# Two blocks of a float32 transformer on one core: first units by halves, a low part in two operations, and one load on another queue

## The reference

```python
def first_block(x, ...):                      # two layers
    x = x + 0.5 * swiglu_ffn(rmsnorm(x), ffn1_wi, ffn1_wo)
    z = rmsnorm(x) @ w_in                     # q, k, v, gates, two output gates ga and gb
    yA = (sigmoid(mo) * rmsnorm(mlstm_chunkwise(...))) @ w_a
    yB = swa_sink_attention(...) @ w_b
    mixed = sigmoid(ga) * yA + sigmoid(gb) * yB
    x = x + mixed @ w_out
    x = x + 0.5 * swiglu_ffn(rmsnorm(x), ffn2_wi, ffn2_wo)
    x = x + sigmoid(rmsnorm(x) @ w_ple_gate) * (p @ w_ple)

def second_block(x, ...):                     # two layers
    uv, z, xbc, dt, c_q, c_kv, k_rope = split(rmsnorm_2(x) @ w_in_2)
    y = [gmlp_mixer(uv), ssd_mixer(z, xbc, dt), mla_mixer(c_q, c_kv, k_rope, cos, sin)]
    x = x + concatenate(y) @ w_out_2
    x = x + square(relu(rmsnorm_2(x) @ mlp_w1)) @ mlp_w2
```

## Time and profile before

| | us |
|---|---|
| median of three executions | 3557.78 |
| profiled execution | 3561.82 |
| its span in the trace | 3560.0 |
| TensorE matmuls busy | 3481.5 |
| TensorE weight loads busy | 2786.3 |
| DVE busy | 1766.3 |
| GpSimd busy | 1402.4 |
| ScalarE busy | 1004.3 |

### The profile page before, as it was taken

The page is one execution under the profiler, slowest core; times in us unless marked ns, Lnnn a source line. Parts: engine busy times, 40 slices in busy tenths (PEclk is TensorE's granted clock), DMA queues, the critical chain, the costliest instruction groups (busy, mean ns, idle before and its releaser), DMA issues.

```text
span 3560.0 us, 42975 instructions
## 1 busy us (share of the span) xinstructions
PE 3481.5 (98%) x15538; PEld 2786.3 (78%) x15538; DVE 1766.3 (50%) x2059; ACT 1004.3 (28%) x1290; POOL 1402.4 (39%) x583
## 2 busy tenths in 40 slices
PE   8999999999999999999999999999999999999998
PEld 7888876788888788887678888776788887578887
DVE  5442246654424643133765442568481826848171
ACT  3222233222222322223422222333321123342112
POOL 3444432344443444433234444331244443134442
PEclk9999999999999999999999999999999999999999
DMA  4333322233332333332123333321233323123332
GB/s 143 95 94 101 107 73 58 71 89 100 99 102 84 100 100 95 107 88 77 55 77 95 99 95 103 93 69 34 66 92 97 94 92 85 30 66 101 95 100 78
DMA packets 496142, 311.26 MB, mean 87 GB/s; under 512 B 41784, under 2 KB 454811, under 8 KB 496027
## 3 DMA queue, kind: packets, MB, share of 16 engines
q1 hardware_dynamic: 494460, 307.47, 29.4%
q10 hardware_dynamic: 1567, 2.18, 0.2%
HBM read 305.94 MB, written 3.67 MB: 87 GB/s over the span
## 4 chain that ended last, share of the span: by engine, by line
issue 45%; PE 31%; POOL 20%; DVE 3%; DVEq 1%; POOLq 1%; ACT 0%; DMA 0%; ACTq 0%
POOL wl L480 20%; PE bank L517 5%; PE bank L521 4%; PE bank L498 4%; PE bank L503 4%; PE bank L502 4%; PE bank L523 4%; PE bank L1104 1%; PE mb L1131 1%; PE bank L524 1%; PE mb L568 1%; PE mb L1047 1%; DVE sd_p L2124 0%; POOLq L479 0%; DVE xl L1644 0%
## 5 line engine op out<-in xcount | busy, mean ns | idle before, releaser
L480 POOL TENSOR_TENSOR wl<-raw,wh 128x1024 fp32r<-128x1024 f32 x576 | 1401.6, 2435 | 2119.6 <-ACT wh L1258 2119.5
L1258 ACT ACTIVATE wh<-raw 128x1024 fp32r<-128x1024 f32 x576 | 608.0, 1057 | 1616.0 <-PE bank L498 723.7
L517 PE MATMUL bank<-xh,wh 128*128 128x512 f32 x2400 | 940.9, 392 | 0.0
L521 PE MATMUL bank<-xl,wh 128*128 128x512 f32 x2400 | 936.1, 390 | 0.0
L523 PE MATMUL bank<-xh,wl 128*128 128x512 f32 x2100 | 819.4, 390 | 0.0
L517 PEld LDWEIGHTS bank<-xh,wh 128*128 128x128 f32 x2400 | 451.8, 188 | 102.7 <-issue 9.0
L521 PEld LDWEIGHTS bank<-xl,wh 128*128 128x128 f32 x2400 | 452.0, 188 | 92.8
L498 PE MATMUL bank<-hh,wh 128*128 128x512 f32 (+1 forms) x1216 | 473.2, 389 | 0.0
L503 PE MATMUL bank<-hh,wl 128*128 128x512 f32 (+1 forms) x1216 | 473.0, 389 | 0.0
L502 PE MATMUL bank<-hl,wh 128*128 128x512 f32 (+1 forms) x1216 | 473.0, 389 | 0.0
L523 PEld LDWEIGHTS bank<-xh,wl 128*128 128x128 f32 x2100 | 395.5, 188 | 83.0
(11 more groups left out here) (383 smaller groups left out, 3292.4 us busy)
## 6 DMA issues: line engine op xcount, KB each, us to landing
raw<-in_ffn_wi_dram SPq DMA_DIRECT2D x176, 512.0 KB, 3.7
raw<-in_mlp_w_dram SPq DMA_DIRECT2D x128, 512.0 KB, 3.7
raw<-in_w_in_dram SPq DMA_DIRECT2D x102, 512.0 KB, 3.6
raw<-in_ffn_wo_dram SPq DMA_DIRECT2D x88, 512.0 KB, 3.6
raw<-in_w_out_dram SPq DMA_DIRECT2D x32, 512.0 KB, 3.8
raw<-in_w_ple_gate_dram SPq DMA_DIRECT2D x16, 512.0 KB, 3.7
raw<-in_w_a_dram SPq DMA_DIRECT2D x8, 512.0 KB, 3.3
raw<-in_w_b_dram SPq DMA_DIRECT2D x8, 512.0 KB, 3.3
```

Of the source, the lines that this page charges most:

```text
L480: gp.tensor_tensor(wl[j][:], raw[j % RAW_SLOTS][:], wh[j][:].bitcast(F32), ALU.subtract)\
L517: first = pe.matmul(out[0:width, :], h[:, c:c + width], rh[:, k, :], start=k == 0, stop=False)
L521: pe.matmul(out[0:width, :], h[:, c:c + width], rl[:, k, :], start=False, stop=False)
L1258: act.activation(wh[n % SPLIT_SLOTS][:], raw[n % RAW_SLOTS][:], ACT.Copy).then_inc(s.hi_ready, 1)
```

## The change

Three edits. First, the output projection's units 0 to 3 are written out by halves, in the manner of `first_units` without the sum of squares; each of the eight waits for `mixed_ready` stands in unit 0 of its half. Units 4 to 7 stay plain, and without a wait. Second, GpSimd's subtraction of a slab is two operations of 128x512 with one increment behind the second. Third, the wait on line 385 is gone, and the table's load stands on ScalarE's queue in block 2's first layer, behind the four gelus of `gmlp`.

```diff
@@ sync @@
-            sp.wait_ge(s.tile_evacuated, tiles_out(Block1, 1, T_PLE + 5))
-            sp.dma_start(rope[:], a["rope_pack"]).then_inc(s.rope_landed, 16)
@@ gpsimd @@
                     gp.wait_ge(s.hi_ready, n * SPLIT_SLOTS + j + 1)
-                    gp.tensor_tensor(wl[j][:], raw[j % RAW_SLOTS][:], wh[j][:].bitcast(F32), ALU.subtract)\
-                      .then_inc(s.split_done, 1)
+                    for half in range(2):
+                        part = slice(half * (SLAB // 2), (half + 1) * (SLAB // 2))
+                        last = gp.tensor_tensor(wl[j][:, part], raw[j % RAW_SLOTS][:, part], wh[j][:, part].bitcast(F32),
+                                                ALU.subtract)
+                    last.then_inc(s.split_done, 1)
@@ tensor, gated @@
-                for j in range(KT):
-                    unit(Block1, L, S_OUT + j, T_OUT + j, mh, ml, part_ready=s.mixed_ready,
-                         wait_k=(lambda k: at(L, KT, k + 1)) if j == 0 else None)
+                for half in range(2):
+                    for u in range(4):
+                        n = S_OUT + u
+                        if not half:
+                            take_slab(Block1, L, n)
+                            open_tile(Block1, L, T_OUT + u)
+                        out = bank[(Block1.base_tile + T_OUT + u) % TILE_BANKS][:]
+                        h, l = wh[n % SPLIT_SLOTS], wl[n % SPLIT_SLOTS]
+                        for kt in range(4 * half, 4 * half + 4):
+                            if u == 0:
+                                pe.wait_ge(s.mixed_ready, at(L, KT, kt + 1))
+                            c = kt * P
+                            last = three(out, h[:, c:c + P], l[:, c:c + P], mh[:, kt, :], ml[:, kt, :], kt == 0,
+                                         kt == KT - 1, new=kt == 4 * half and (u > 0) == (half > 0))
+                        if half:
+                            last.then_inc(s.tile_ready, 1)
+                for j in range(4, KT):
+                    unit(Block1, L, S_OUT + j, T_OUT + j, mh, ml)
@@ scalar, gmlp of block 2 @@
                     act.activation(proj2[:, u, :], proj2[:, u, :], ACT.Gelu_apprx_tanh)
+                if L == 0:
+                    act.dma_start(rope[:], a["rope_pack"]).then_inc(s.rope_landed, 16)
                 act.drain()
```

## The result

The changed kernel takes 3528.83 us (median of 6 runs, 3519.3 to 3533.68) where the kernel before took 3556.24 (6 runs, 3553.79 to 3559.77): a ratio of 0.992, 95% interval 0.991 to 0.9929, or about 28 us less. The forecast was 3537, 8 us above it; the measured time lies 0.8 us inside the lower end of the forecast's range of 3528 to 3549. The run profiled took 3528.16 us, its span is 3526.4.

The account below looks back on a forecast made before the run. TensorE, busy 98% of the span, bounds the kernel by its work plus waits. Terms -13.8 - 6.8 + 0 = -20.6 us give 3541.2 from the profiled execution, 3537 by the median; range 3528 to 3549.

Parts of the forecast that it names:

- The projection by halves: Block 1's output projection, both layers: waits for the mixed tiles' low part and half-clock time go, -13.8 us.
- The bank's wait: Output projection, unit 2: opening its bank waits for DVE's read of tile 6; 1.15 us a layer, between 0.8 and 2.
- The first rival: Output projection: openings of units 1 to 3 wait longer and the clock falls; 3543 us, chance 0.13.
- The table's move: Seam between blocks 1 and 2: slab loads no longer queue behind the table's wait on SP; -6.8 us.
- The third rival: Second seam: moving the table's load does nothing, as slab rounding or another load holds it; 3544 us, chance 0.08.
- The split: GpSimd's low parts in two operations: gains and costs where TensorE waits for DVE cancel; 0 us, between -8 and +10.
- The seams: `xl` before the sum of squares, both seams: one waiting operation ends sooner with halved low parts, -0.9 us x 2.
- The chains: Successive waiting DVE operations let GpSimd in once more: logits' scalings +0.3 us at four waits, scan heads' products and query +0.3 x 2.
- The scan: Block 2's first layer: a single DVE operation waiting for GpSimd ends sooner with halved low parts, -1.15 us.
- The added operation: GpSimd's second operation per slab: 0.1 us more a slab at some ten places where TensorE waits on DVE.
- The slower rival: Attention and scan stages: splitting low parts lengthens TensorE's path by 0.45 us at about 80 slabs; 3573 us, chance 0.08.
- the second, 3527: Rival that splitting low parts gains at every place, DVE never meeting the second half; 3527 us, chance 0.10.

Follow-up runs that it names:

- e3: Only the rotary table's load moved to ScalarE's queue, against the kernel before: 3545.18 us, ratio 0.9976.
- e8: All three edits, but the table loaded on SP's queue behind block 2's first four slabs and the gMLP parameters, against the kernel before: 3529.84 us, ratio 0.9923.
- e4: Projection by halves and table's load moved, low parts left whole, against the kernel before: 3537.94 us, ratio 0.9948.
- e10: The changed kernel, all three edits, run again against the kernel before: 3526.57 us, ratio 0.9918.
- e1: Only the output projection's first four units by halves, against the kernel before: 3544.58 us, ratio 0.9966.
- e11: All three edits, but low parts in four uneven operations of 512, 480, 16 and 16 columns, against the kernel before: 3527.38 us, ratio 0.9916.
- e12: All three edits, but low parts in eight operations of 128x128, against the kernel before: 3518.97 us, ratio 0.9897.
- e9: All three edits, but low parts in four operations of 128x256, second run of that kernel, against the kernel before: 3519.57 us, ratio 0.9894.
- e7: All three edits, but low parts in four operations of 128x256, first run of that kernel, against the kernel before: 3521.27 us, ratio 0.9899.

## Why the prediction was off, step by step

**The projection by halves: right, to its size.** -13.8 was forecast, 12 measured alone (7 to 17). In the pair of profiles the four units lose 7.45 us less in the first layer and 7.67 in the second. The bank's wait is 0.8 us without the split and 0.2 with it, where I had taken 1.15 a layer. The first rival, banks that take back a part and lower the clock, did not come about: the windows show 1.00.

**The table's move: right.** -6.8 against 9 (5 to 12) alone, and both seams run alike. The third rival, that it does nothing, falls by e3 and e8. With the halves beside it the two terms made -20.6, and e4 measured 18 (14 to 23). Both are covered by what was argued. As they fell short by 2 to 3 us, if by anything, the whole miss of 8 us lies in the third term.

**The split: this step failed.** I took its term at 0, and it brought 6 us alone (2 to 9) and 9 to 11 beside the others. The term was made of TensorE's waits for VectorE, -0.6 in sum, and of 0.1 us a slab at ten places. Time at the lower clock, which the projection's term had in it, was left out of this one. As a sum of waits it was not far off: from e4 to e10 TensorE stands still for 1.0 us less, and its busy time falls by 5.7 (table below). By that pair of profiles, most of what the split brought is in what the sum left out. Place by place the list of waits came out differently, too.

*The seams* were to gain 0.9 us each, from one waiting operation. Timeline, the kernel after, ahead of the reduction at the first seam:
```profile
1153.86 1.64 DVE L1662 SCALAR_TENSOR_TENSOR xl<-x_sb,p,xh 128x512 fp32r<-128x512 f32 x1
1155.42 1.51 DVE L1660 TENSOR_SCALAR xh<-x_sb,p 128x512 fp32r<-128x512 f32 x1
```
One `xl` of 2.74 us has become two waiting operations. TensorE's waits for the sum's input are 2.52 and 2.49 us where they were 1.97 and 3.08: together no shorter.

*The chains* were to lose 0.3 us each, since GpSimd comes in once more. Timeline, the kernel after, the four scalings of the logits, and the scan of block 2's first layer with GpSimd beside it; last, the operation ahead of the scan in the kernel before:
```profile
647.04 3.27 DVE L1918 TENSOR_SCALAR lg<-lg,small 128x256 f32<-128x256 f32 x4
...
2351.75 2.71 POOL L480 TENSOR_TENSOR wl<-raw,wh 128x512 fp32r<-128x512 f32 x2 [2.98 <-ACT wh L1274]
...
2351.99 1.32 DVE L2093 TENSOR_SCALAR tmp_all<-var,small 6x512 f32<-6x512 f32 x1
2353.38 2.15 DVE L2095 TENSOR_TENSOR_SCAN acc<-ones,tmp_all 6x512 f32<-6x512 f32 x1
```
```profile
2382.69 0.47 DVE L2075 TENSOR_SCALAR tmp_all<-var,small 6x512 f32<-6x512 f32 x1
```
The four scalings take 3.27 us where they took 3.33: no loss in the chain. TensorE's waits for `lg` are 10.3 us in the kernel after, but with whole low parts they are 9.0 in e4 and 10.5 in e1, so they show neither a gain nor a loss. *The scan*, forecast at -1.15, turned into a chain itself: 1.32 + 2.15 = 3.47 us for it and the operation ahead of it, where the two took 0.47 + 3.21 = 3.68, a gain of 0.2. TensorE's waits for the scans' `acc` are 1.2 to 1.7 us in the runs with halves in block 2 and 2.5 to 4.3 in those without. How much of that is the split's is open, since in the kernel before and in e1 this chain also began later, after 1.91 us of waiting for ScalarE.

*The added operation*, 0.1 us a slab at ten places, shows in no median up to four operations: a slab of e11 is 0.44 us longer than one of e10, and the two times are the same, with the reserve made above that a gain may have hidden a loss. The slower rival, 0.45 us a slab straight on the path of 80 slabs, fell: e11 and e12 lengthen slabs by 0.68 and 1.33 us against the kernel before, and both are among the faster kernels. The rival whose time came out is the second, 3527, to which I had given 0.10. Its mechanism did not: it had VectorE never meet the second half, and VectorE meets it at the seams, in the scan and in the subtraction behind the cast. Nor does it name time at the lower clock. That its number comes near is luck.

**Where the gain appears, the forecast only half said.** It counted idle time and the lower clock together only at the projection. From the pages (span, TensorE's busy time, the difference; mean granted clock):

| kernel | span | PE busy | rest | clock |
|---|---|---|---|---|
| before | 3560.0 | 3481.5 | 78.5 | 0.986 |
| halves and table (e4) | 3536.2 | 3472.2 | 64.0 | 0.988 |
| changed again (e10) | 3529.5 | 3466.5 | 63.0 | 0.991 |
| 512, 480, 16, 16 (e11) | 3528.8 | 3471.7 | 57.1 | 0.988 |
| in four (e9) | 3518.8 | 3463.4 | 55.4 | 0.991 |
| in eight (e12) | 3516.1 | 3456.7 | 59.4 | 0.993 |

With the same matmuls in all, the busy time falls as the clock rises, by 24.8 us from 0.986 to 0.993. Neither column tells the time alone: e11 stands idle 6 us less than e10 and pays 5 us more in busy time, and the sums are equal. From e4 to e10 the idle time falls by 1.0 us only and the busy time by 5.7. So what the split saved in this pair of profiles is mostly time at the lower clock. The same holds for e9 against e11: 1.7 us less idle time, 8.3 us less busy time. Why shorter operations of GpSimd leave TensorE less time at the lower clock, these runs do not show. Which of its stretches an execution has is partly its own: the runs of the kernel before lie between clock 0.985 and 0.991, and their times between 3561 and 3548. Why one execution of the same kernel keeps the full clock through a stretch where another loses it (3.4 us in the table of stretches) stays open; no run here was made for it. The pair of profiles that the sum was made on shows 33.7 us, some 5 more than the medians, and this is the reason why a sum on single executions is good to about that.

**GpSimd's fixed cost, and who holds the ports.** By the Trainium skill, page "GPSIMD Engine Reference", section "Elementwise — side-by-side cycle accounting", I had worked out an estimate of 0.37 us for what an operation costs beyond its elements. The trace does not agree: an operation of 16 columns takes 297 ns all told, and each one added to a slab cost 0.24 us (one to two), 0.22 (to four) and 0.16 (to eight). The rows' bound, the copy of 284 ns, held. The rule of the Trainium skill's page "SBUF — State Buffer", section "Who interferes with whom", that the engine which issued first holds the ports for its whole instruction, agrees with e9 and e11: VectorE's cast follows the length of GpSimd's longest operation, 1195 ns beside 1357 and 1168 beside 1320, but 690 beside 808. It gets in between two queued operations, as the start had shown.

## What to carry to other kernels

When one engine's long operations block another's short ones, the length of the longest of them decided here, and cutting it paid until the longer total was itself waited for; measure the cut at two, four and eight parts, and with an uneven cut as the control that separates length from number. Price a chain that meets two halves at about what it took with the one whole wait, its own operations included, unless a row shows more. Count idle time and time at the lower clock as one sum, for every edit, and don't read 5 us of either out of one pair of profiles. A load with a wait in an in-order queue costs what stands behind it: moving it a few entries back on the same queue was worth as much as another queue.

The best version of these runs is all three edits with the low parts in four operations: 3519.57 us, ratio 0.9894 (0.9879 to 0.9909) to the kernel before, 7 us under the changed kernel run beside it (e10), and 3521.27 in e7. Eight parts are level with it.

## What the hardware showed that I had not expected

GpSimd's subtraction and VectorE's cast pay opposite prices: GpSimd's busy time rose from 1402 to 2164 us with eight parts, VectorE's fell from 1766 to 1405, 361 us less with the same 2059 instructions (e4, with the other two edits and whole low parts, has 1769). At least a fifth of VectorE's busy time before was waiting that the page shows as busy. And a cast of 128x512 that stood at 2009 ns in the kernel before takes 456 ns on average beside operations of 506 ns: its own duration is at most that, less than a quarter of what the profile had given for it.
